# Compression of the sparse-attention keys and values moved from a stage of its own into the input projection

## The reference, cut to what matters

```
kc = _partial_rope(_compress(kc_tok, pe_k, w_k1, w_k2, tok_idx), positions[:, cmp_end])
vc = _compress(vc_tok, pe_v, w_v1, w_v2, tok_idx)
...
def _compress(tok, pe, w1, w2, tok_idx):       # 63 windows of 32 tokens, one every 16 tokens
    blk = tok[:, tok_idx] + pe[None, None, :, None, :]
    blk = jnp.swapaxes(blk, 2, 3).reshape(B, n_cmp, NSA_KV_HEADS, CMP_BLOCK * HEAD_DIM)
    return jax.nn.silu(blk @ w1) @ w2
...
log_f = jax.nn.log_sigmoid(f_logit.astype(jnp.float32))     # forgetting attention
cum = jnp.cumsum(log_f, axis=1).transpose(0, 2, 1)
```

## Time and profile before

| | us |
|---|---|
| runs, median of 3 | 1595.18 |
| profiled execution, its own time | 1597.06 |
| profiled execution, its span | 1595.4 |
| TensorE busy | 1397.2 (88%) |
| VectorE busy | 760.9 (48%) |
| ScalarE busy | 629.0 (39%) |
| GpSimd busy | 148.5 (9%) |
| mean granted TensorE clock | 0.941 of full |

### The profile page before, as it was taken

One profiled execution on the slowest core, in us unless ns is written; L12 is line 12 of the kernel. 1 busy time (PEld: TensorE's weight loads), 2 busy tenths in 40 slices (PEclk: granted clock), 3 DMA queues, 4 the chain that ended last, 5 costly groups with the idle time before them and its releaser, 6 DMA issues. The chain is left out here.

```text
span 1595.4 us, 24135 instructions
## 1 busy us (share of the span) xinstructions
PE 1397.2 (88%) x7996; PEld 1167.6 (73%) x7997; DVE 760.9 (48%) x1240; ACT 629.0 (39%) x930; POOL 148.5 (9%) x146
## 2 busy tenths in 40 slices
PE   4999999737999999999969964999999999628997
PEld 3777889735899989888858854777777777516774
DVE  6633012235444444434254235678654767626552
ACT  6211110013333333445443212567644657515442
POOL 0000000013111112322000000010000000011000
PEclk9999999967999999999979975999999999858999
DMA  5122321144000012354033215799877979464410
GB/s 185 55 75 93 118 75 35 36 104 97 21 21 22 21 46 57 81 125 93 12 121 115 83 53 203 285 331 389 315 253 243 375 259 377 180 237 158 137 49 39
DMA packets 107988, 222.48 MB, mean 139 GB/s; under 512 B 14749, under 2 KB 41405, under 8 KB 107910
## 3 DMA queue, kind: packets, MB, share of 16 engines
q1 hardware_dynamic: 96950, 183.07, 35.4%
q0 software_dynamic: 7488, 27.27, 4.8%
q10 hardware_dynamic: 3472, 11.09, 1.7%
HBM read 176.56 MB, written 36.24 MB: 133 GB/s over the span
## 5 line engine op out<-in xcount | busy, mean ns | idle before, releaser
L1178 ACT ACTIVATE att_prob<-att_ps_s 128x512 f32<-128x512 f32 (+1 forms) x240 | 134.7, 562 | 246.2 <-PE att_ps_s L1105 201.3
L1227 DVE TENSOR_REDUCE att_mx<-att_ps_m 128x1 f32<-128x512 f32 (+3 forms) x256 | 132.8, 560 | 135.0 <-PE att_ps_m L1052 123.2
L1924 DVE TENSOR_TENSOR moe_g_lo<-moe_g_raw,moe_g_hi 128x1024 fp32r<-128x1024 f32 x128 | 148.1, 1218 | 45.5 <-ACT moe_g_hi L1844 44.8
L135 PE MATMUL moe_ps_g<-moe_g_hi,moe_xT_hi 128*128 128x512 f32 x336 | 137.7, 410 | 17.8 <-DVE moe_g_lo L1924 17.7
L1844 ACT ACTIVATE moe_g_hi<-moe_g_raw 128x1024 fp32r<-128x1024 f32 x128 | 124.9, 1047 | 44.4 <-PE moe_ps_g L137 24.4
L1123 PE MATMUL att_ps_o<-tok_vsw,att_prob 128*128 128x65 f32 x1056 | 140.1, 274 | 0.0
L136 PE MATMUL moe_ps_g<-moe_g_lo,moe_xT_hi 128*128 128x512 f32 x336 | 134.3, 400 | 0.0
L137 PE MATMUL moe_ps_g<-moe_g_hi,moe_xT_lo 128*128 128x512 f32 x336 | 133.9, 399 | 0.0
L1123 PEld LDWEIGHTS att_ps_o<-tok_vsw,att_prob 128*128 128x128 f32 x1056 | 131.2, 192 | 2.6 <-ACT att_prob L1178 0.5
L135 PE MATMUL prj_ps_w<-prj_hT_hi,prj_w_hi 128*128 128x512 f32 x256 | 103.0, 402 | 3.0 <-DVE prj_w_lo L405 3.0
L136 PE MATMUL prj_ps_w<-prj_hT_lo,prj_w_hi 128*128 128x512 f32 x256 | 100.3, 392 | 0.0
(11 more groups left out here) (339 smaller groups left out, 2909.8 us busy)
## 6 DMA issues: line engine op xcount, KB each, us to landing
moe_g_raw<-in_w_gate_e SPq DMA_DIRECT2D x128, 256.0 KB, 4.9
moe_g_raw<-in_w_up_e SPq DMA_DIRECT2D x128, 256.0 KB, 6.2
moe_d_raw<-in_w_down_e SPq DMA_DIRECT2D x64, 512.0 KB, 7.6
y_rows<-moe_y ACTq DMA_DIRECT2D x21, 512.0 KB, 6.1
prj_w_raw<-in_w_in SPq DMA_DIRECT2D x16, 512.0 KB, 4.0
att_q_raw<-feat SPq DMA_DIRECT2D x32, 256.0 KB
feat<-att_w_out POOLq DMA_DIRECT2D x14, 512.0 KB, 2.9
att_k_raw<-feat SPq DMA_DIRECT2D x24, 256.0 KB
```

What stands on the lines that cost most here:

```text
L135: nc.tensor.matmul(out, a_hi, b_hi, start=first, stop=False)
L1178: nc.scalar.activation(prob[:, b % PT, 0:w], ps_s[:, b % ST, 0:w], ACT.Exp, scale=-1.0).then_inc(expd, 1)
L1227: last = nc.vector.tensor_reduce(mx[i % 2][:, col, q:q + 1], p[:, at:at + (kb - ka) * P], X, ALU.min)
L1924: nc.vector.tensor_tensor(g_lo[:, ch % GR], g_raw[:, ch], g_hi[:, ch % GR].bitcast(F32), ALU.subtract).then_inc(s_glo, 1)
```

## The change

`stage_compress` is gone; its work is inside `stage_project`.

- Order of the start: SP loads the first 512 columns of the constants early and the rest late; the first two blocks of `w_in` are split by ScalarE after tiles 1 and 3, and their low parts by GpSimd instead of VectorE. TensorE does block 0 for the first 512 tokens (`early_half(0, 0)`) after tile 3, block 1 for them after tile 5, and the second halves after tile 7. `ps_w` is then one bank for each block.
- The copy out of these two blocks (`early_out`) writes the tokens sorted by their place in the stride, so that eight DMAs on the GpSimd queue can build `win` in which the columns of each product adjoin. `w1` and the small tensors are loaded on the GpSimd queue too, the second half of `w1` after those eight.
- The split of block 2 on VectorE stands ahead of the range reduction (`wrap`) of the trigonometry instead of behind it.
- The 2 x 16 products follow the rotations of blocks 4 and 5, the second products the block 7, the rotation of the compressed keys the block 7's rotation.
- The chunk with gates and forget logits comes first of the three; the log-sigmoid, running sum and gates are done by VectorE behind the copies out of the other two chunks, by ScalarE behind the splits of the second, and TensorE transposes the forget logits ahead of the second chunk.
- The barriers and the semaphore clearing of `stage_compress` are gone.

The removed stage is printed above; of the rest this is the core:

```diff
+        win = [K["o"][:, 2:5, :].rearrange("p a n -> p (a n)")[:, kv * GROUPS * HW:(kv + 1) * GROUPS * HW].rearrange(
+            "p (g j n) -> p g j n", g=GROUPS, j=JP) for kv in range(2)]
+        tokT = K["tokT"].rearrange("p a (h j n) -> p a h j n", h=2, j=JP)
+        w1 = [K["o"][:, n:n + 2, :].rearrange("p a n -> p (a n)").rearrange("p (m n) -> p m n", n=P) for n in (5, 0)]
...
+        fT, fe, cum, ones = (K["o"][0:NH, n, :] for n in (5, 6, 0, 1))
+        cum_hi, cum_lo = (t[0:NH, 0].rearrange("p k n -> p (k n)") for t in (w_hi, w_lo))
+        ps_f = ps_x[0:NH].rearrange("p a n -> p (a n)")
+
+        def hid_of(kv):
+            return ps_x[:, kv, 0:GROUPS * N_WIN].rearrange("p (g n) -> p g n", g=GROUPS)
...
-        VCH = [[(C_VB, 256)], [(C_VB + 256, 256)], [(C_VS, 128), (C_VW, 128), (C_GATE, 24), (C_F, 8)]]
+        VCH = [[(C_VS, 128), (C_VW, 128), (C_GATE, 24), (C_F, 8)], [(C_VB, 256)], [(C_VB + 256, 256)]]
...
+                x_tile(0)
+                sp.dma_start(gain[:], a["g_mix"].to_broadcast((P, D))).then_inc(gain_in, 16)
+                sp.dma_start(K["c"][:, 0:K_DIAG], a["consts"][:, 0:K_DIAG]).then_inc(const_in, 16)
+                x_tile(1)
+                w_first(0)
+                x_tile(2)
+                x_tile(3)
+                w_first(1)
+                x_tile(4)
+                x_tile(5)
+                sp.dma_start(K["c"][:, K_DIAG:K_COLS], a["consts"][:, K_DIAG:K_COLS]).then_inc(const_in, 16)
+                x_tile(6)
+                sp.dma_start(pos, a["positions"].to_broadcast((P, S))).then_inc(pos_in, 16)
+                x_tile(7)
...
+                sp.wait_ge(hid_made, 2)
...
+                for s in range(2):
+                    pool.wait_ge(split_hi, s + 1)
+                    nc.gpsimd.tensor_tensor(w_lo[:, s], w_raw[:, s], w_hi[:, s].bitcast(F32),
+                                            ALU.subtract).then_inc(split_lo, 1)
+                    pool.wait_ge(split_lo, s + 1)
...
+                pool.dma_start(w1[0], w1_d[0]).then_inc(w1_in, 16)
...
+                pool.wait_ge(evac, 4)
+                for kv in range(2):
+                    for g in range(GROUPS):
+                        for h in range(2):
+                            pool.dma_start(win[kv][h * HD:(h + 1) * HD, g, :, 0:S // CMP_STRIDE],
+                                           tokT[g * HD:(g + 1) * HD, kv, h]).then_inc(win_in, 16)
+                pool.wait_ge(win_in, 128)
+                pool.dma_start(w1[1], w1_d[1]).then_inc(w1_in, 16)
...
+                def early_out(n, h):
+
+                    act.wait_ge(product, 2 * h + n + 1)
+                    w = S // CMP_STRIDE // 2
+                    nc.scalar.activation(tokT[:, n, :, :, h * w:(h + 1) * w],
+                                         ps_w[:, n, :].rearrange("p (n j h) -> p h j n", j=JP, h=2),
+                                         ACT.Copy).then_inc(evac, 1)
...
+                    if t in (1, 3):
+                        s = t // 2
+                        act.wait_ge(w_in_[s], 16)
+                        nc.scalar.activation(w_hi[:, s], w_raw[:, s], ACT.Copy).then_inc(split_hi, 1)
+                    if t in (5, 7):
+                        early_out(t // 2 - 2, 0)
...
+                    if row is None:
+                        early_out(n, 1)
+                    else:
+                        for h in range(2):
+                            copy_out(n % 2, h, 2 * n + h + 1, 16 * stores_before(n) or None,
+                                     -SCALE if row < 4 else 1.0)
+                    split((16 * (n // 2 + 2), 2 * n + 2 if n else 3), n % 2)
+                    if n == 6:
+                        act.wait_ge(bias_copied, 1)
+                        for kv in range(2):
+                            nc.scalar.activation(hid[:, 2 * kv:2 * kv + 2, 0:N_CMP], hid_of(kv)[:, :, 0:N_CMP],
+                                                 ACT.Sigmoid, bias=bias[:, kv:kv + 1]).then_inc(hid_sig, 1)
...
+                    if n == 1:
+                        act.wait_ge(fe_made, 1)
+                        nc.scalar.activation(fe, fe, ACT.Exp).then_inc(f_exp, 1)
+                        act.wait_ge(gate_added, 1)
+                        nc.scalar.activation(K["gate"][:], K["gate"][:], ACT.Exp, scale=-1.0).then_inc(g_exp, 1)
+                        act.wait_ge(f_exp, 1)
+                        nc.scalar.activation(fe, fe, ACT.Ln, bias=1.0).then_inc(f_ln, 1)
...
-                for s in range(2):
-                    split(s, s + 1)
...
+                split(0, 3)
                 wrap(ang)
...
-                split(0, 3)
...
+                def compress(n):
+
+                    if n == 2:
+                        dve.wait_ge(pe_turned, 1)
+                        for kv in range(2):
+                            for g in range(GROUPS):
+                                nc.vector.tensor_copy(win[kv][:, g, :, S // CMP_STRIDE:],
+                                                      ps_b[:, kv * PAIRS:(kv + 1) * PAIRS].rearrange(
+                                                          "p (c j) -> p j c", c=2)).then_inc(pe_copied, 1)
+                    if n == 5:
+                        dve.wait_ge(hid_made, 2)
+                        nc.vector.tensor_copy(bias, ps_x[:, :, N_WIN - 1]).then_inc(bias_copied, 1)
+                        dve.wait_ge(bias_copied, 1)
+                    if n == 6:
+                        for kv in range(2):
+                            dve.wait_ge(hid_sig, kv + 1)
+                            h = hid[:, 2 * kv:2 * kv + 2, 0:N_CMP]
+                            nc.vector.scalar_tensor_tensor(h, hid_of(kv)[:, :, 0:N_CMP], bias[:, kv:kv + 1], h, ALU.add,
+                                                           ALU.mult).then_inc(hid_act, 1)
...
                 halves = 0
                 for n, (_, _, rope) in enumerate(FIXED):
+                    if n == NFIX - 1:
+                        compressed_out()
...
+                    compress(n)
+                compressed_rope()
...
+                compressed_in()
...
+                    if t == 6:
+                        dve.wait_ge(f_ln, 1)
+                        dve.wait_ge(fe_made, 1)
+                        cmp_step(nc.vector.tensor_tensor(fT, fT, fe, ALU.subtract))
+                    if t == 7:
+                        cmp_step(nc.vector.tensor_tensor_scan(cum, ones, fT, 0.0, ALU.mult, ALU.add))
+                    if t == 8:
+                        dve.wait_ge(product, 4 * NFIX)
+                        cmp_step(nc.vector.tensor_copy(cum_hi, cum))
+                        nc.vector.tensor_tensor(cum_lo, cum, cum_hi.bitcast(F32), ALU.subtract).then_inc(cum_made, 1)
...
+                        if n:
+                            gates((n - 1) * NT + t)
...
+                def early_half(s, h):
+
+                    if h == 0:
+                        pe.wait_ge(split_hi, s + 1)
+                        pe.wait_ge(split_lo, s + 1)
+                    else:
+                        pe.wait_ge(evac, s + 1)
+                    pe.wait_ge(up_lo, NT * (h + 1))
+                    for k in range(KD):
+                        last = mm3(nc, ps_w[:, s, :], w_hi[:, s, k, :], w_lo[:, s, k, :],
+                                   hT_hi[:, k, h * 512:(h + 1) * 512], hT_lo[:, k, h * 512:(h + 1) * 512],
+                                   k == 0, k == KD - 1)
+                    last.then_inc(product, 1)
+
+                for t in range(4):
+                    turn(t)
+                early_half(0, 0)
+                turn(4)
+                turn(5)
+                early_half(1, 0)
+                turn(6)
+                turn(7)
+                early_half(0, 1)
+                early_half(1, 1)
...
+                    if n in (4, 5):
+                        kv = n - 4
+                        pe.wait_ge(w1_in, 16 * (kv + 1))
+                        if kv == 0:
+                            pe.wait_ge(pe_copied, 4)
+                            pe.wait_ge(win_in, 128)
+                        for m in range(PAIRS):
+                            cols = win[kv][:, :, m % JP, m // JP:m // JP + N_WIN]
+                            last = nc.tensor.matmul(hid_of(kv), w1[kv][:, m, :], cols, start=(m == 0),
+                                                    stop=(m == PAIRS - 1))
+                        last.then_inc(hid_made, 1)
...
+                    if n == 1:
+                        pe.wait_ge(v_evac, NT)
+                        for t in range(NT):
+                            last = nc.tensor.transpose(ps_f[:, t * P:(t + 1) * P], K["gf"][:, t, 24:32], ident)
+                        last.then_inc(f_turned, 1)
...
-                stage_compress(nc, a, K, T)
```

More of the change, by code:

```diff
@@ L252, in _, with x_tile @@
             def _(sp):
[L253 to L256, removed]
+                def x_tile(t):
                     if t >= XR:
@@ L336, in copy_out @@
                         act.wait_ge(stored[s], stored_at)
```

(43 more changed lines are left out.)

281 lines of the change are left out of this document (100 added, 181 removed).

## The result

The changed kernel takes 1572.05 us (median of 4 runs, 1571.11 to 1573.89) against 1595.48 before (median of 4); the ratio is 0.9852, 95% interval 0.9834 to 0.9869: 23.4 us less. The profiled execution took 1571.11 with a span of 1569.4, 26.0 less than the span before. Forecast was 1567 with a range of 1559 to 1577.

What follows compares the result with a forecast made beforehand. Bound: TensorE in most of the projection, VectorE in its first part, plus a 42 us serial stage. Terms -42.0 + 7.1 + 4.1 (other TensorE work) + 2.3 = -28.5 took 1595.2 to 1567 us, range 1559 to 1577.

Steps and rivals of the forecast that it cites:

- The stage that goes: Between the projection's last copy and attention's first DMA: 43.4 us shrinks to one border of 1.4, removing 42.0 us.
- The 2 x 16 products: 64 instructions on TensorE between a rotation and the next block, 0.111 us each with adjoining columns: +7.1 us.
- Rival C: The 2 x 16 products keep the strided price of 0.20 us each: +5.7, 1572.5 us; chance 0.11.
- The first part: Projection start through block 2: the early halves bring nothing, block 2 ends at 75.0 against 72.7: +2.3 us.
- the hold by GpSimd: At the start, GpSimd's subtraction holds VectorE's multiply of tile 3: +1.0 us (0 to 2.3).
- the stop in block 2: TensorE stands 5.1 us before block 2's second half, awaiting a copy out queued behind the sines; lower clock adds 2.1.
- The chunks: V chunks: the running sum adds 2.0 us of TensorE wait ahead of the third, eight transposes 0.3 ahead of the second.
- GpSimd's queue: Window copies, second `w1` and block 2's store: 6144 runs at 4.2 ns issue in 25.6 us, just fitting; cost 0.
- B: The GpSimd queue is late at 7.6 ns a run, TensorE stands 18.8 us: 1586 us; chance 0.12.
- D: The GpSimd queue, its issue locked against VectorE, stalls TensorE beyond the gain: 1600 us at 10 ns a run; chance 0.03.
- Rival A: The early halves pay: VectorE isn't held, the clock stays up, tile 1 comes earlier: 1562.6 us; chance 0.2.
- E: The change fails, for example the removed stage's idle time returns at the start of attention: 1595 us; chance 0.02.

Runs made afterwards that it cites:

- the distance run: Changed kernel with the 2 x 16 products reading wrong columns, 1 and 2 values apart for keys, 4 and 8 for values; 1631.8 us, one execution, total not comparable.

## Why the prediction was right, step by step

The mechanism and the direction hold, and the time lies in the range, 5 us above the forecast.

- **The stage that goes**, -42.0: exact. From the last copy's end (325.68 + 0.42) to attention's first DMA it is 1.43 us, forecast 1.4; the added semaphores cost nothing to be seen.
- **The 2 x 16 products**, 7.1: right. The half block behind a rotation, 8.3 us from copy to copy else, is 11.88 and 11.89 where the products stand (104.03 to 115.91, 121.34 to 133.23): 3.6 each. Rival C is out, and the distance run shows that C's price was the distance. The price itself was misread: a window also counts instructions that began ahead of it, so 20 in 4 us is not 0.20 each. From start to start it was 0.22, and C would have cost 7.0 us, not 5.7.
- **The first part.** The first early half was forecast at 24.6 and starts at 24.61, with errors in its terms that cancel: ScalarE gets to tile 1 1.1 us earlier (9.38 against 10.47), where I took 1.65, and the hold by GpSimd was half of the 1.0 I took (it lengthens the 1.28 us by 0.54 and 0.62). GpSimd's instruction lay beside the multiply for only 0.75 and 0.82 us; a longer overlap would have cost more. VectorE is through with tile 7 at 45.17, forecast 45.9; the stop in block 2 was forecast at 5.1 and is 4.8. That the early halves bring nothing was right and too mild: by the run that undoes them, they and the moved split together cost 4.65 us (6.0 at block 2). Mis-sized is the half (0, 1): from 45.31 to 52.6, 7.3 against 5.4 forecast, at a granted clock of 0.59 to 49.5, after 1.56 us of waiting and a stretch of thin work (2.37 us busy in 41 to 46). The forecast had it only among its bounds. It is no fixed cost: the clock fell there in five of seven profiles with the same code ahead.
- **The chunks**: the term that failed. The wait ahead of the third chunk was right (3.59, forecast about 4), that ahead of the second was free (1.9 us lie between the chunks there as before, and the eight transposes fill them). But I let the chunks themselves run as before. After waits of 2.1 and 3.6 us two of them begin with 3.4 and some 3 us at half clock: from low parts to last copy 28.3 and 25.5 us, where the same widths took 26.8 and 23.9 before: 1.5 each. Filling the waits removed 2.9. The rule I had used for block 2, that a wait of that length costs the clock, I did not apply here, because the wait before the change was nearly as long (2.02) and did no harm. The row the rule came from doesn't carry it either: at 382, behind the 2.6 us wait, the clock was at half, but it had been at half ahead of that wait too.

```profile
380.00:381.00 1.00, 0.10 (x1) 0.00 (x0) 0.00 (x0) 0.98 (x2) 0.00 (x0) 0.50 0.00 0
```

In block 2 the clock did fall, inside the wait of 4.8 us. The length of a wait alone does not decide: the same 2.14 us were followed by half clock in six profiles and not in the seventh, while the 3.59 us ahead of the last chunk were in all six. What else decides is open.

- **GpSimd's queue**, 0: right, and with much room. Taken at 4.2 ns a run, it was 5.87/4096 = 1.4 and 1.16/2048 = 0.6: most of the issue price is by the DMA, little of it by its runs (0.57 for 128, 0.69 for 512, 1.16 for 2048). The store of block 2 left at 81.3 and landed 8.1 us later; the copy out that needs it came at 98.59. Rivals B and D are out. D's mechanism is there, but small: beside VectorE's scaling the first window copy took 1.13 us to issue in place of 0.69.
- **Sum**: forecast -28.5, at attention's first DMA -25.2. Of the 3.3 missing, 3.0 are the clock in two chunks, 0.9 the first part; some 0.6 of the small terms came out lower. The rest between 25.2 and the 23.4 of the medians is within the spread of what follows the projection.
- **Rival A** (the early halves pay): false, and also where the clock held in half (0, 1): in the distance run block 2's second copy came at 75.02, 2.1 later than before the change. E (the removed time returns): false.

## What to carry to other kernels

Work moved ahead of a phase that another engine paces can delay that engine's next long task; look up what that task gates before counting the gain. Here a copy out queued behind two sines cost more than the early work brought, and either swapping the two or dropping the early work was worth 4 to 5 us. The stage between two barriers was worth its full length minus what TensorE had to do of its work elsewhere. Waits left on TensorE should be charged with the clock as well, as a range: the 3.6 us wait cost 5 to 6, the 2.1 us wait 3.6 in most profiles and 2.1 in one.

## What the runs showed of the hardware

- A float32 product appears as two instructions. With 130 moving columns each costs 0.22 to 0.24 us when the columns lie 16, 32 or 64 bytes apart, and 0.11 to 0.12 at 4 and 8 bytes, at full clock. At half clock the distance cost nothing: the 64-byte ones stayed at 0.22 (11 instructions in the window 330 to 332 at clock 0.50, and 11 in 334 to 336 at 1.00, kernel before), and eight transposes of 128 adjoining columns took 1.97 us at 1429.56, at 0.50 too.
- The granted clock went from 2.4 to 1.2 GHz 1.3 and 0.3 us after the products had begun again behind waits of 2.1 and 3.6 us; with the early halves undone it fell inside the 3.6 us wait (0.50 in 294.4 to 295.3, products from 295.35), as it did in the 4.8 us wait of block 2. It stayed there for 2.8 to 3.4 us of full work in most profiles and for 5.8 and 6.0 us of it in two. Sixteen transposes of 0.12 us in the 2.1 us wait kept it at 2.4 in both profiles that had them.
- A GpSimd subtraction (2.36 us) lengthened a VectorE operation with two inputs in SBUF by 0.54 and 0.62 us, while the two lay side by side for 0.75 and 0.82 us. A VectorE reduction out of PSUM beside such a subtraction was not lengthened (0.69 us at 367.15, as at 388.21 in the kernel before, where GpSimd was idle).
- VectorE held the issue of a DMA on the GpSimd queue by 0.44 us (1.13 in place of 0.69), beside an operation on the sine and cosine in SBUF.
